# Sliding-window attention layer: value projection with the weights as stationary operand, logits spread over four quarters of the TensorE array

## What is computed

```python
def swa_mixer(h, w_in, b_in, sinks, rel_bias, w_out):
...
    proj = h @ w_in + b_in
    q = proj[..., :SWA_QD].reshape(B, N, CHUNK, SWA_HKV, SWA_GROUP, SWA_HD)
    k = proj[..., SWA_QD:SWA_QD + SWA_KD].reshape(B, S, SWA_HKV, SWA_HD)
    v = proj[..., SWA_QD + SWA_KD:SWA_QD + 2 * SWA_KD].reshape(B, S, SWA_HKV, SWA_HD)
    gate = proj[..., SWA_QD + 2 * SWA_KD:]
...
    logits = jnp.einsum('bnqhgd,bnkhd->bnhgqk', q, kb).astype(jnp.float32) * (SWA_HD ** -0.5)
...
    m = jnp.maximum(jnp.max(logits, axis=-1, keepdims=True), sink)
    e = jnp.exp(logits - m)
    p = e / (jnp.sum(e, axis=-1, keepdims=True) + jnp.exp(sink - m))
    out = jnp.einsum('bnhgqk,bnkhd->bnqhgd', p.astype(h.dtype), vb).reshape(B, S, SWA_QD)
    y = out * jax.nn.silu(gate)
    return y @ w_out
```

## Time and profile before

| | |
|---|---|
| median of 3 runs | 3475.66 us (3473.05 to 3478.53) |
| span of the profiled execution | 3470.1 us |
| mean granted TensorE clock | 0.987 |
| PE busy | 3346.7 us, 96% |
| DVE, ACT, POOL busy | 68%, 44%, 28% |

### The profile page before, as it was taken

The page is one execution under the profiler, slowest core; times in us unless marked ns, Lnnn a source line. Parts: engine busy times, 40 slices in busy tenths (PEclk is TensorE's granted clock), DMA queues, the critical chain, the costliest instruction groups (busy, mean ns, idle before and its releaser), DMA issues.

```text
span 3470.1 us, 50530 instructions
## 1 busy us (share of the span) xinstructions
PE 3346.7 (96%) x19519; PEld 2716.4 (78%) x19519; DVE 2344.9 (68%) x3772; ACT 1539.2 (44%) x2765; POOL 961.0 (28%) x495
## 2 busy tenths in 40 slices
PE   6999999999999999999979999999999999999998
PEld 3777788877887778888867777888778877788887
DVE  5886788766568867556567777896536664666555
ACT  5666566333344124322466655653334431342334
POOL 1004343111143124222510052432111521422253
PEclk8999999999999999999989999999999999999999
DMA  5432265456843612111231123554449221221113
GB/s 175 135 114 71 72 173 137 131 158 191 306 154 101 194 58 85 50 31 37 80 133 52 48 80 87 157 138 127 129 128 340 80 61 49 67 74 32 37 49 103
DMA packets 569020, 383.91 MB, mean 111 GB/s; under 512 B 67802, under 2 KB 522445, under 8 KB 568781
## 3 DMA queue, kind: packets, MB, share of 16 engines
q1 hardware_dynamic: 568781, 380.68, 36.5%
HBM read 299.01 MB, written 80.54 MB: 109 GB/s over the span
## 4 chain that ended last, share of the span: by engine, by line
PE 73%; DVE 13%; ACT 4%; DMA 3%; issue 3%; SPq 2%; POOL 2%; PEldq 0%; ACTq 0%; DVEq 0%; PEld 0%; POOLq 0%
PE bank L236 55%; DVE dnp_conv L1929 3%; PE bank L255 2%; DVE dnp_diag_inv L2003 2%; DMA dn_planes<-dnp_inv_t 1%; PE bank L2464 1%; PE bank L2675 1%; DVE dnp_diag_term L2000 1%; PE bank L2716 1%; PE bank L2702 1%; DVE h_lo L748 1%; DVE pool_ada_sums L302 1%; POOL w_lo L218 1%; PE bank L2230 1%; PE bank L2690 1%
## 5 line engine op out<-in xcount | busy, mean ns | idle before, releaser
L236 PE MATMUL bank<-h_hi,w_hi 128*128 128x512 f32 x3488 | 1414.8, 406 | 23.1 <-DVE x_res L805 5.6
L236 PE MATMUL bank<-h_hi,w_lo 128*128 128x512 f32 x3488 | 1367.5, 392 | 0.0
L236 PE MATMUL bank<-h_lo,w_hi 128*128 128x512 f32 x3488 | 1366.3, 392 | 0.0
L218 POOL TENSOR_TENSOR w_lo<-w_raw,w_hi 128x1024 fp32r<-128x1024 f32 x262 | 649.4, 2480 | 1337.2 <-ACT w_hi L209 1336.5
L236 PEld LDWEIGHTS bank<-h_hi,w_hi 128*128 128x128 f32 x3488 | 659.5, 189 | 188.9 <-issue 27.7
L236 PEld LDWEIGHTS bank<-h_lo,w_hi 128*128 128x128 f32 x3488 | 660.2, 189 | 141.3 <-issue 12.7
L236 PEld LDWEIGHTS bank<-h_hi,w_lo 128*128 128x128 f32 x3488 | 659.1, 189 | 142.7
L209 ACT ACTIVATE w_hi<-w_raw 128x1024 fp32r<-128x1024 f32 x292 | 307.8, 1055 | 344.7 <-PE bank L236 238.4
L1929 DVE SCALAR_TENSOR_TENSOR dnp_conv<-dnp_raw,dn_conv_w,dnp_conv 128x512 f32<-128x512 f32 x288 | 259.6, 901 | 188.2 <-ACT dnp_conv L1742 181.0
L127 POOL TENSOR_TENSOR h_lo<-y,h_hi 128x512 fp32r<-128x512 f32 x72 | 112.2, 1571 | 504.6 <-ACT h_hi L118 504.0
L775 DVE TENSOR_TENSOR res_sq_total<-res_sq_total,res_sq 128x512 f32<-128x512 f32 x140 | 156.0, 1114 | 55.7 <-ACT res_sq L896 55.0
(11 more groups left out here) (343 smaller groups left out, 4825.9 us busy)
## 6 DMA issues: line engine op xcount, KB each, us to landing
dnr_in<-dn_planes SPq DMA_DIRECT2D x112, 512.0 KB, 7.0
dn_planes<-y SPq DMA_DIRECT2D x192, 256.0 KB, 2.6
w_raw<-in_dn_w_in SPq DMA_DIRECT2D x64, 512.0 KB, 4.6
y<-in_ada_w SPq DMA_DIRECT2D x80, 256.0 KB, 4.9
w_raw<-in_swa_w_in SPq DMA_DIRECT2D x36, 512.0 KB, 3.6
w_raw<-in_rg_w_in SPq DMA_DIRECT2D x32, 512.0 KB, 4.5
w_raw<-in_rg_w_out SPq DMA_DIRECT2D x32, 512.0 KB, 3.5
w_raw<-in_dn_w_out SPq DMA_DIRECT2D x32, 512.0 KB, 3.4
```

Of the source, the lines that this page charges most:

```text
L218: alu.tensor_tensor(self.lo[j % SLOTS][:, :, :], self.raw[j % 2][:, :, :], self.hi[j % SLOTS][:, :, :].bitcast(F32), ALU.subtract).then_in ...
L236: ins = self.nc.tensor.matmul(out, w[slot][:, k, :], x[:, k, cols], start=(k == 0 and n == 0), stop=(k == KT - 1 and n == 2))
```

## The change

**Values.** `w.multiply` now makes them with the weights stationary, 24 matmuls per chunk. The result has value columns on partitions. ACT adds the bias and copies it to `sil[c]` (borrowed), PE turns it in four transposes (`turn_values`, to banks 7 and 5), and DVE copies it to `vals`. The value-bias tile and its DMA go.

**Logits.** The output partition half is chosen by the block's parity instead of the head, and the bank by the head. So the same matmuls run, but on four quarters of the array (64 rows by 64 columns) instead of two. `lg`'s second axis becomes head, pair of blocks, so DVE adds the bias in two operations of 512 columns instead of six, and sinks are read per head.

**Bias tile.** It must now hold both heads on both partition halves, with the swapped order for even blocks: 1 MB instead of 512 KB. Half of it (`relb_early`, pairs 0 to 3) lies in the last slice of `y`, which is free until late; twelve DMAs load it instead of two, six before the key copies and six behind them, ahead of the weight tiles. The preparing copies of DVE (`vals_even`, carried keys and values) move behind the first unit's subtraction.

```diff
-                pe.wait_ge(w.split, tile0 + 2)
-                for b in range(BU * c, BU * c + BU):
-                    for k in range(KT):
-                        for m, (x, ww) in enumerate(((h_hi, w.hi), (h_hi, w.lo), (h_lo, w.hi))):
...
+                w.multiply(pe, bank[3 + 3 * c][:, :], tile0 + 1, h_hi, h_lo, slice(c * CH, c * CH + CH))
...
+            def turn_values(c):
+
+                pe.wait_ge(s["v_copied"], c + 1)
+                for b in range(BU):
+                    ins = nc.tensor.transpose(bank[VT_BANKS[c]][:, b * P:b * P + P], sil[c][:, b * P:b * P + P],
+                                              core.ident[:, :])
+                ins.then_inc(s["v_turned"], 1)
...
-                        out = bank[3 + j // 4][rows, j % 4 * P:j % 4 * P + P]
...
+                for i in range(NW // 2):
+                    for parity in range(2):
+                        at = (c * NW + 2 * i + parity) * QW
+                        half_rows = slice(parity * QW, parity * QW + QW)
+                        for b in range(2):
+                            rows = slice(b * HD, b * HD + HD)
+                            q = qs[rows, (2 * i + parity) * QW:(2 * i + parity) * QW + QW]
+                            out = bank[3 + b][half_rows, i * P:i * P + P]
...
+                act.wait_ge(w.projected, prod0 + 3 * c + 2)
+                nc.scalar.activation(sil[c][:, :], bank[3 + 3 * c][:, :], ACT.Identity, bias=vbias).then_inc(s["v_copied"], 1)
             w.round_to(act, tile0 + 4)
...
+                    for b in range(2):
+                        V.tensor_tensor(lg[c][:, 4 * b:4 * b + 4, :], bank[3 + b][:, :].rearrange("p (i k) -> p i k", i=4),
+                                        bcast_mid(rel_bias(n)[:, b, :], 4), ALU.add).then_inc(s["logits"], 1)
...
+                    if unit == 1:
+                        arrange_values()
                     dve.wait_ge(s["exp"], unit)
```

More of the change, by code:

```diff
@@ L2621, in swa_phase, with skewed, rel_bias @@
         table = core.swa_table
-        def skewed(b):
-            return bass.AP(tensor=table.tensor, offset=table.offset + b * QW * REL + QW - 1,
-                           ap=[[REL - 1, QW], [2 * QW * REL, KT], [1, 2 * QW]])
+        def skewed(first, b, key, count):
+            at = table.offset + (2 * first + b) * QW * REL + QW - 1 + key
+            return bass.AP(tensor=table.tensor, offset=at,
+                           ap=[[REL - 1, QW], [2 * QW * REL, KT // 2], [1, count]])
+        def rel_bias(n):
+            return (relb_early if n < KT // 2 else relb_late)[:, n % (KT // 2), :, :]
         @block.sync
@@ L2634, in _, with load_bias @@
             sp.dma_start(sink[:, :], A["swa_sinks"].partition_broadcast(P)[:, 0, :]).then_inc(s["vectors"], 16)
-            vb = A["swa_b_in"][:, QD + KD:QD + 2 * KD]
-            sp.dma_start(vbias[:, :], vb.partition_broadcast(P)[:, 0, :]).then_inc(s["vectors"], 16)
             sp.wait_ge(core.table_stored, 16)
-            for b in range(2):
-                sp.dma_start(relb[b * QW:b * QW + QW, :, :], skewed(b)).then_inc(s["bias"], 16)
+            def load_bias(dst, first):
+                for parity in range(2):
+                    rows = slice(parity * QW, parity * QW + QW)
+                    for b in range(2):
+                        if parity:
+                            sp.dma_start(dst[rows, :, b, :], skewed(first, b, 0, 2 * QW)).then_inc(s["bias"], 16)
+                            continue
+                        for i in range(2):
+                            sp.dma_start(dst[rows, :, b, i * QW:i * QW + QW], skewed(first, b, QW - i * QW, QW))                                .then_inc(s["bias"], 16)
+            load_bias(relb_early, 0)
             sp.wait_ge(s["keys"], 4)
@@ new lines, in logits @@
+            def logits(kv, c):
+                for i in range(NW // 2):
+                    for parity in range(2):
+                        at = (c * NW + 2 * i + parity) * QW
[4 more added lines that the diff above has]
+                            out = bank[3 + b][half_rows, i * P:i * P + P]
+                            if parity:
+                                ins = nc.tensor.matmul(out, q, kk[kv][rows, at:at + 2 * QW], start=True, stop=True)
+                            else:
+                                nc.tensor.matmul(out[:, 0:QW], q, kk[kv][rows, at + QW:at + 2 * QW], start=True, stop=True)
+                                nc.tensor.matmul(out[:, QW:P], q, kk[kv][rows, at:at + QW], start=True, stop=True)
@@ L2721, in _ @@
             pe.wait_ge(s["carried"], 3)
-            pe.wait_ge(s["values"], 1)
             for u in range(units):
@@ L2728, in _ @@
                     w.multiply(pe, bank[0][:, :], tile0 + 2 + 2 * n, h_hi, h_lo, cols)
+                    if u == 1:
+                        pe.wait_ge(s["values"], 2)
                     turn(u, (c + 1) % NCH)
@@ L2748, in last_weigh @@
                 core.leave(pe, "pe")
-            pe.wait_ge(s["logits"], 6 * units)
+            pe.wait_ge(s["logits"], 2 * units)
             core.pe_tail = {KT - 3: last_turn, KT - 1: last_weigh}
@@ L2814, in _ @@
             V.tensor_copy(par[:, :, 2], bg).then_inc(s["par"], 1)
-            dve.wait_ge(s["vectors"], 32)
-            by_pair = sink[:, :].rearrange("p (n b) -> p n b", b=2)
-            for i in range(2):
-                rows = slice(i * QW, i * QW + QW)
-                V.tensor_copy(par[rows, :, 3], by_pair[rows, :, i]).then_inc(s["par"], 1)
-            dve.wait_ge(s["par"], 5)
+            dve.wait_ge(s["par"], 3)
             V.tensor_copy(cur[:, :], par[:, 0, :]).then_inc(s["cur"], 1)
```

85 lines of the change are left out of this document (38 added, 47 removed).

## The result

| | before | after |
|---|---|---|
| median of the runs | 3477.1 us (3473.05 to 3480.01, 4 runs) | 3449.71 us (3448.53 to 3450.36, 4 runs) |
| span of the profiled execution | 3470.1 us | 3446.7 us |
| mean granted TensorE clock | 0.987 | 0.982 |

The ratio is 0.9922, with a 95% interval of 0.9911 to 0.9934: 27.4 us less. The prediction was 3445.9 us, in a range of 3436 to 3457, against a median of before that was 1.4 us lower at the time. Direction, size and range held. The two terms of its sum didn't hold alike, and the rest of this document is about that.

The account below looks back on a forecast made before the run. PE was taken to bound the attention layer, its logits by the array quarters used. Units 25.5 us plus start 4.3 us made 29.8 us off the 3475.7 us median: 3445.9 us, range 3436 to 3457.

Parts of the forecast that it names:

- The two terms of its sum: Attention layer: 25.5 us saved by shorter logits in 30 units, plus 4.3 us net at the start of both halves.
- Logits: Logits matmuls in each unit: four quarters take 0.23 us a pair instead of 0.46, saving 0.85 us a unit.
- The open point: Logits: whether tiles with the same output partitions, head 0 and head 1 in banks 3 and 4, run beside each other.
- The look ahead: Logits: PE takes a free quarter's work from at least four records behind; 0.27 us a pair with four, 0.23 with ten.
- Units: Attention units after each half's first: 30 units get 0.85 us shorter each, 25.5 us in all (22 to 27).
- Start: Start of each half: values save 10.35 us, PE then waits for the query; net 4.3 us in all, -2 to +11.7.
- The clock's 1.2 us: Start of each half: the lower clock after PE's 5.7 us wait costs 1.2 us net, about a third hidden under POOL.
- the 5.6 us between span and median: Whole program: the difference between profiled span 3470.1 us and median 3475.7 us, taken to stay.
- The rest at nothing: DVE's bias operations, moved preparing copies (0.8 us of cover left) and late bias tile: no cost or gain counted.
- Taking turns: Rival in the logits: tiles with the same output partitions don't overlap, units gain nothing; 3471.4 us, chance 7%.
- draining: Rival in the logits: each change of stationary rows drains work under way, 1.3 us more a unit; 3509 us, chance 4%.
- The third: Rival at the start: SP's issues are short, the tile lands early, start gives 13 us or more; 3436 us, chance 5%.

Follow-up runs that it names:

- lower_quarters: The changed kernel with every logits matmul writing to partitions 0 to 63, so on two quarters instead of four; 3475.0 us, ratio to before 0.9998.
- evens_then_odds: The changed kernel with the two logits loops exchanged, all four even blocks ahead of all four odd ones; 3469.6 us, ratio to before 0.9977.
- by twos: The changed kernel with its logits in the order two even blocks, two odd blocks in turn; 3458.2 us (one run).
- the values alone: The kernel before with only the new values projection, its logits, bias tile and two bias DMAs kept; 3468.3 us, ratio to before 0.9978.

## Why the prediction was right, and where its steps were off

**Logits: right.** The step from the earlier trace rows, that a quarter takes a new record of 64 columns every 0.058 us and that it is the quarter that bounds, gave 0.23 us a pair; measured is 0.23. The open point (same output partitions, other bank) came out as the earlier trace rows suggested, and lower_quarters shows it by itself. The look ahead was put at "at least four records"; the rows show odd records that pass five even ones not yet begun (evens_then_odds) and six (the changed kernel's unit). The prediction's 0.27 us a pair for a look of four doesn't come out when it is played through again with the same figures: four, and even three, give 0.23, two give 0.34. So the lower bound of 0.73 us a unit was set by a wrong sum, and the measured 0.23 a pair doesn't tell four from more; the other orders do. The saving in the logits is 0.83 us, near the 0.85 that I took.

**Units: 23.7 us instead of 25.5.** The term left out is behind the logits: the gate product that follows takes 0.04 us longer than before. I had nothing for it in the sum. 0.79 a unit lies inside the stated 0.73 to 0.90.

**Start: 1.8 us instead of 4.3**, in the range of -2 to 11.7. The mechanism was the one forecast (SP's twelve bias issues, PE waiting for `swa_q` behind `w_hi`), the sizes were off. The gate tile's DMA went out 10.8 us behind the sinks; I had 1414.6 - 1405.2 = 9.4. Most issues took 0.62 to 0.66 us as taken, but the second one in each burst 1.13 to 1.19, and the fixed gaps added up. Landing took 4.42 instead of 4.1. In the other half one burst alone had a long issue (1.09), the DMA went out 10.1 us behind the sinks and landed after 4.11. So PE waited 7.6 and 6.7 us instead of 5.7. The clock's 1.2 us are right as a mean of two unlike halves. The first gate product began 0.3 us behind POOL's end in both (1426.95 against 1424.31 + 2.36 = 1426.67 in the first), so at full clock it could have begun that much earlier, and the 48 matmuls behind it took 11.69 and 12.64 us instead of 11.2: 0.8 and 1.7 us.

**The number.** Part of its nearness is luck. The sum was 29.8 us; the layer gave 25.4, the medians differ by 27.4 and the profiled executions by 23.4. The prediction also kept the 5.6 us between span and median, which were not a constant: after the change they are 3449.7 - 3446.7 = 3.0.

**The rest at nothing: right.** DVE's preparing copies stand in the first unit's chain and there POOL ends at 1435.08 + 1.90 = 1436.98, with the turn at 1438.47: 1.5 us of cover instead of 0.8, the later start included. No engine has a new wait in the units.

**The rivals.** Taking turns (3471) and draining (3509) are ruled out by the 1.13 us. The third, a start that gives all of it (3436), was not what the change does, but what it could have done: with the gate tile first the kernel reaches 3432.6. I had named the place, the chain behind the twelve issues, and priced the start at 13 us or more; it is worth 31.4 + 31.4 - 22.1 - 21.5 = 19.2, of which the change itself has 1.8. What kept it from that is the order of SP's queue and the length of its issues, the point that the prediction set against this rival.

## What to carry to other kernels

Small matmuls (here 64 rows by 64 columns) gain by the number of quarters that have work close together in program order: choose the partition of the result (not only of the operands) so that neighbours use different quarters, and interleave them at the finest grain. When a matmul stage gets shorter at the start of a phase, look at what the DMA queue issues first: here six transfers that nobody needed for 100 us stood ahead of the one that everybody waited for. Taking that one ahead of them was worth some 5 us, taking it to the head of the whole queue and rounding it early 17. A wait of PE can cost more than its length: behind waits of 3.7 to 7.6 us the next 48 matmuls took 11.7 to 13.2 us instead of 11.2, and shortening the wait by 3 us gave back 1.6 us in one place and 2.9 in another.

## What the runs showed of the hardware that I had not expected

- Matmuls of the four quarters don't start in program order: odd records began up to six even ones early (1454.40, where L2709's begin at 1454.54). The Trainium skill, "TensorE: Matmul & The Clock Gate" (The mechanism), has them start and end strictly in order, with a window of 64 for weight loads; the traces here disagree with the order of starts, and by twos (sixteen even records in a group) the overlap was already incomplete, 1.39 against 1.17 us.
- The low clock had the same end, near 1428, whether PE took work up again at 1421.8 or at 1424.9; both had last worked at 1417.3. In the other half it was back before 3108 with work from 3102.2 on, and still low up to 3110 with work from 3105.6 on. With the wait filled by transposes it didn't fall at all.
- A weight tile issued right behind the key copies landed after 5.55 us (5.56 with the values alone), one issued behind six bias DMAs after 4.42 us, although more was queued ahead of it.
- In most bursts of bias DMAs one issue, mostly the second, took 1.0 to 1.7 us on SP, most others 0.60 to 0.66. The first of a burst took 1.9 to 2.5 us where two weight tiles had been issued just ahead of it, and the first burst of the other half had no long issue in nine of ten kernels. I don't know why.
